# Second mixer of a two-block transformer kernel: an earlier gate chunk, a later second block set, earlier key parts and first scaling, an earlier retention score, later merge transfers

## Chip, cores and metric

The kernel runs on one core of one Trainium2 chip, as a single launch. The metric is the device time of that launch in microseconds (us), the median of three runs. The engines are PE (TensorE, matrix products), DVE (VectorE), ACT (ScalarE), POOL (GpSimd) and SP (SyncE, which here only issues transfers).

## Reference

Two transformer blocks over a sequence of 512 tokens of width 1024, all in fp32. The second block, where the change lies, is a half-weighted SwiGLU, a mixer, a second half-weighted SwiGLU and a norm. Its mixer, cut to what matters:

```python
h = _rmsnorm(x, mix_norm)
(q_a, kc_a, vc_a, ks_a, vs_a, kw_a, vw_a, g_a, q_r, k_r, v_r, g_r, g_merge) = jnp.split(h @ w_in, ...)
nsa_gates = jax.nn.sigmoid(g_a...)
# sparse attention: keys and values of 31 overlapping blocks of 32 tokens, compressed by a small MLP
def compress(tok, w1, w2):
    blk = tok[:, :, cmp_idx] + pos_emb
    return jax.nn.gelu(blk.reshape(...) @ w1) @ w2
kc = _rope(compress(k_cmp, ck_w1, ck_w2), cmp_end); vc = compress(v_cmp, cv_w1, cv_w2)
# scores of q on kc, the key blocks that score best, attention on those and on a window, gated sum
a_out = _nsa(...)
# retention: causal products of q_r and k_r with a decay, times v_r, group norm, times silu(g_r)
r_out = jax.nn.silu(g_r) * _retention(q_r, k_r, v_r, gain)
gate_a, gate_r = jnp.split(jax.nn.sigmoid(g_merge), 2, axis=-1)
x = x + (gate_a * (a_out @ w_branch_nsa) + gate_r * (r_out @ w_branch_ret)) @ w_out
```

## The kernel before

**Products.** Every fp32 product is made of three matmuls on high and low parts (`mm3`, L177 to L179). Activations lie as 8 tiles of 128 x 512 (`xn_hi`, `xn_lo`), and the weights come as a stream of 337 chunks of 512 KB.

**The stream.** SP loads a chunk into one of two buffers `w_raw`; the load of chunk n waits until the low part of chunk n-2 is made. ACT makes the high part (`high_part`, L146, into `w_hi`, a ring of four; it waits for the load and until PE has used chunk n-4). DVE makes the low part (`low_part`, L151, into `w_lo`; it waits for the high part). PE's `ready` waits for the low part. `ahead(part, eng, first, j)` makes the part of chunk first + j + 2. Each engine works through its own list in the order in which the code issues it, so that an instruction that waits holds back all that is behind it on its engine.

**Chunks of the second mixer**, in the order of use: two for the compressed tokens (`b2_cmp`), two for values (`fv`), one for the gates (`fg`), then sixteen called fm+0 to fm+15, two `fk`, and the rest. fm+2c is a chunk of query or key projections (`kq_chunk(c)`, 24 matmuls of 512 columns), fm+2c+1 one of the compressing MLP (8 matmuls of 256 columns on `blk_parts`, L1647 and L1649). `kq_chunk(8)` and `kq_chunk(9)` use the `fk` chunks.

**The start of the mixer.** DVE makes the normed tiles (L224), ACT their high parts (L216), POOL their low parts (L232); this is `scaled_parts`. ACT then copies the compressed tokens across partitions (`ck`, L1553). From `ck` DVE adds the position embedding into `blk`, eight instructions for the keys (`blocks(0)`) and eight for the values (`blocks(1)`), all at L1721. ACT makes the high parts of `blk` (`blocks_high`, L1674), POOL the low parts (L1778). `blk` is cleared on POOL at L1775. The gates are the product with `fg`, a sigmoid on ACT (`gate_fm`, L1681), and a transpose on PE (L1633).

**Rotation.** After `kq_chunk(n)` DVE shuffles and multiplies its bank (L1747, L1749 or L1753, "rotation n" below), and POOL multiplies and adds the sines (L1782, L1787 or L1792). The low parts of the next two chunks stand on DVE ahead of rotation n.

**First scores.** The compressed keys `kc_raw` get high parts on ACT (`high_kc`, L1967) and low parts on POOL (`low_kc`, L2012). PE then makes small scores on them and the first score on the window (L183, L184), runs `kq_chunk(9)`, makes the next score, and transposes the scaled probabilities (L1881). DVE scales those by the gates (`scaled`, L2189 to L2199). `low_q`, `low_k`, `low_v` (L1997, L2005, L2018) are POOL's low parts for queries, keys and values.

**Retention and merge.** In the retention `fill(h, ...)` runs a chunk's matmuls in two parts, and `score(1)` and `values(0)` are products that need parts of the rotated queries and keys (`rk_lo`, POOL L2326). In the merge gates come back from DRAM in four pairs of transfers on POOL's queue (L2633) and `x` in one of 2 MB on ACT's (L2585).

Of the kernel before, what the change touches and what calls it, by code (L numbers as in the profile page):

```python
# [25 lines left out]
S = 512  # L26
# [53 lines left out]
def build_program(nc, stream, xt, cols, tables, rows, decays, pos, w2, out):  # L80
    top = ExitStack()
    with top:
# [125 lines left out]
        def scaled_parts(gain):  # L208
# [4 lines left out]
            def act_part(act):  # L213
                for k in range(KT):
                    act.wait_ge(m["scaled"], b["scaled"] + k + 1)
                    nc.scalar.activation(xn_hi[:, k, :], squares[:, k % 4, :], ACT.Copy).then_inc(m["hi"], 1)  # L216
                    if k == KT // 2:
                        ahead(high_part, act, FIRST["b2_cmp"], 1)

# [1281 lines left out]
        def mixer2(n_mix2, x_done, last_sum, recip_done, opened):  # L1501
# [7 lines left out]
            def tables_in(pool):  # L1509
                pool.wait_ge(*x_done)  # L1510
# [147 lines left out]
            def act_part(act):  # L1658
# [17 lines left out]
                for j in range(2):  # L1676
                    ahead(high_part, act, fv, j)
                ahead(high_part, act, fg, 0)
                blocks_high(0)
                finished(act, fg, 0)  # L1680
                nc.scalar.activation(gate_fm[0:48, :], banks[3][0:48, :], ACT.Sigmoid).then_inc(t["gate"], 1)  # L1681
                for c in range(8):
                    if c == 1:
                        blocks_high(1)
                    ahead(high_part, act, fm, 2 * c)
                    ahead(high_part, act, fm, 2 * c + 1)
# [11 lines left out]
                    if c == 7:  # L1698
                        act.wait_ge(t["kc"], 4)
                        high_kc(0)  # L1700
                        cross_q(act, 0)
# [7 lines left out]
            def dve_part(dve):  # L1709
# [14 lines left out]
                for j in range(2):  # L1724
                    ahead(low_part, dve, fv, j)
                ahead(low_part, dve, fg, 0)
                blocks(0)
                finished(dve, fv, 1)
                for tb in range(TB):
                    nc.vector.tensor_copy(nv[:, tb, :], banks[4 + tb][:, 0:256]).then_inc(t["v"], 1)  # L1730
                blocks(1)
                dve.wait_ge(t["tables"], 128)
                nc.vector.tensor_tensor(fold, ident[:, 0:64], ident[:, 64:P], ALU.add)
                for n in range(10):
# [6 lines left out]
                    for c in ((2 * n, 2 * n + 1) if n < 8 else (n - 8,)):  # L1741
                        ahead(low_part, dve, fm if n < 8 else fk, c)
                    finished(dve, *place_of(n))
# [29 lines left out]
            def pool_part(pool):  # L1773
                pool.wait_ge(*norm_done)
                nc.gpsimd.memset(blk[:], 0.0).then_inc(consts_made, 1)  # L1775
                for kv in range(2):
# [36 lines left out]
        def sparse_attention(start):  # L1813
# [361 lines left out]

            def first_shift(dve):
                compressed_shift(dve, 0)
                biased(dve, 0)

            def dve_part(dve):  # L2180
                dve.wait_ge(t["pad"], 1)
                dve.wait_ge(t["gates"], 1)

                def scaled(U):

                    i, (j, m) = U // 4, units[U % 4]
                    n = slice(4 * (U % 2), 4 * (U % 2) + 4)
# [679 lines left out]
```

## Time and profile before

| what | value |
|---|---|
| median of three runs | 2178.33 us (2175.91 to 2180.74) |
| time of the profiled execution | 2178.4 us |
| its span | 2176.6 us |
| PE busy | 2128.0 us, 98% of the span |
| DVE, ACT, POOL busy | 1188.5, 895.4, 461.5 us |
| second mixer to merge | from about 1120 to 1760 us of the span |

PE is busy for 98% of the span. A stretch is read by asking where PE stands idle, which engine let it go on, what that engine did before, and which clock PE was granted after the idle time. A busy PE at a granted clock of 0.50 does half the work in the same time.

### The profile page before, as it was taken

The page shows a single profiled execution, that of the slowest core. Times are in us where ns is not written, and L with a number is a line of the kernel's source. Part 1 is how long each engine was busy: PE and PEld are TensorE (multiplying, and loading weights), DVE is VectorE, ACT ScalarE, POOL GpSimd, SP SyncE. Part 2 cuts the span into 40 slices and gives each one's busy share as a digit, 9 for nine tenths or more (in the row PEclk, how much of TensorE's full clock was granted, in tenths as well). Part 3 has the DMA queues.
Part 4 walks back from the last instruction along what each step waited for, and adds up shares of the span by engine and source line. Part 5 has one row for each costly group of instructions (what it writes and reads, how often), then busy time and mean ns, then how long its engine had stood idle before and what let it go on. Part 6 is the DMA issues. An engine that isn't in the chain of part 4 may idle for free.

```text
span 2176.6 us, 28422 instructions
## 1 busy us (share of the span) xinstructions
PE 2128.0 (98%) x9960; PEld 1762.4 (81%) x9960; DVE 1188.5 (55%) x1981; ACT 895.4 (41%) x1542; POOL 461.5 (21%) x359
## 2 busy tenths in 40 slices
PE   8999999999999999999998899999999999999997
PEld 6778888888888888888887788888877788888886
DVE  5467774544442264443277678778768335444324
ACT  4355664422221242222133467676655424222212
POOL 2011344211110042310015501111155313111000
PEclk9999999999999999999999999999999999999999
DMA  5212245333333333333324322222264432333331
GB/s 169 78 54 73 83 144 161 91 93 96 96 106 101 92 87 96 96 96 106 97 91 153 108 60 77 83 73 69 92 201 179 147 97 87 97 96 96 108 97 66
DMA packets 66505, 222.91 MB, mean 102 GB/s; under 512 B 7312, under 2 KB 7568, under 8 KB 66032
## 3 DMA queue, kind: packets, MB, share of 16 engines
q1 hardware_dynamic: 51120, 182.08, 27.9%
q10 hardware_dynamic: 11712, 27.27, 3.4%
q0 software_dynamic: 3584, 12.39, 1.7%
q8 instruction: 54, 0.88, 0.2%
q14 instruction: 35, 0.29, 0.0%
HBM read 202.31 MB, written 18.87 MB: 102 GB/s over the span
## 4 chain that ended last, share of the span: by engine, by line
PE 83%; DVE 8%; POOL 3%; ACT 2%; issue 2%; DMA 2%; DVEq 0%; SPq 0%; POOLq 0%; ACTq 0%
PE bank L177 24%; PE bank L178 24%; PE bank L179 24%; PE bank L183 3%; PE bank L184 2%; POOL hid L541 2%; PE bank L1881 2%; DVE gn_r L2480 1%; DMA w_raw<-stream 1%; DVE w_lo L151 1%; DVE xn_lo L456 1%; ACT w_hi L146 1%; PE bank L677 1%; DMA m_more<-spill_g 1%; DVE squares L224 0%
## 5 line engine op out<-in xcount | busy, mean ns | idle before, releaser
L151 DVE TENSOR_TENSOR w_lo<-w_raw,w_hi 128x1024 fp32r<-128x1024 f32 x337 | 463.9, 1380 | 536.3 <-ACT w_hi L146 535.9
L177 PE MATMUL bank<-xn_hi,w_hi 128*128 128x512 f32 x1624 | 648.1, 399 | 7.0 <-DVE w_lo L151 6.8
L179 PE MATMUL bank<-xn_hi,w_lo 128*128 128x512 f32 x1624 | 634.9, 391 | 0.0
L178 PE MATMUL bank<-xn_lo,w_hi 128*128 128x512 f32 x1624 | 634.6, 391 | 0.0
L146 ACT ACTIVATE w_hi<-w_raw 128x1024 fp32r<-128x1024 f32 x337 | 353.2, 1051 | 391.5 <-PE bank L179 236.3
L177 PEld LDWEIGHTS bank<-xn_hi,w_hi 128*128 128x128 f32 x1624 | 307.1, 189 | 71.0 <-DVE w_lo L151 7.7
L179 PEld LDWEIGHTS bank<-xn_hi,w_lo 128*128 128x128 f32 x1624 | 305.9, 188 | 64.9
L178 PEld LDWEIGHTS bank<-xn_lo,w_hi 128*128 128x128 f32 x1624 | 306.7, 189 | 62.6 <-issue 2.6
L177 PE MATMUL bank<-h_hi,w_hi 128*128 (+1 forms) x528 | 205.8, 390 | 0.0
L179 PE MATMUL bank<-h_hi,w_lo 128*128 (+1 forms) x528 | 205.4, 389 | 0.0
L178 PE MATMUL bank<-h_lo,w_hi 128*128 (+1 forms) x528 | 205.4, 389 | 0.0
L547 POOL TENSOR_TENSOR h_lo<-hid,h_hi 128x512 f32 (+1 forms) x66 | 85.6, 1297 | 564.6 <-ACT h_hi L407 564.6
L407 ACT ACTIVATE h_hi<-hid 128x512 f32 (+1 forms) x66 | 41.7, 632 | 290.4 <-DVE hid L477 290.4
L178 PEld LDWEIGHTS bank<-h_lo,w_hi 128*128 128x128 f32 x528 | 99.1, 188 | 20.9 <-issue 0.2
L177 PEld LDWEIGHTS bank<-h_hi,w_hi 128*128 128x128 f32 x528 | 99.1, 188 | 20.7 <-issue 0.2
L179 PEld LDWEIGHTS bank<-h_hi,w_lo 128*128 128x128 f32 x528 | 99.1, 188 | 20.7
L403 ACT ACTIVATE silu<-silu 128x512 f32<-128x512 f32 x66 | 41.6, 631 | 174.5 <-DVE silu L467 174.5
L473 DVE TENSOR_TENSOR hid<-bank,norm_r 128x512 f32<-128x512 f32 x66 | 45.6, 690 | 112.1 <-PE bank L179 112.1
L2066 ACT ACTIVATE npt_hi<-bank 128x512 fp32r<-128x512 f32 (+3 forms) x128 | 48.6, 431 | 70.9 <-PE bank L1881 70.9
L2037 ACT ACTIVATE nprob<-nprob,small 128x128 f32<-128x128 f32 (+3 forms) x128 | 70.8, 555 | 16.9 <-DVE small L2173 16.4
L2205 DVE TENSOR_TENSOR npt_lo<-bank,npt_hi 128x512 fp32r<-128x512 f32 (+3 forms) x128 | 56.7, 484 | 35.2 <-ACT npt_hi L2066 35.2
L467 DVE TENSOR_TENSOR silu<-bank,norm_r 128x512 f32<-128x512 f32 x66 | 45.6, 691 | 45.2 <-PE bank L179 45.1
(414 smaller groups left out, 3120.5 us busy)
## 6 DMA issues: line engine op xcount, KB each, us to landing
w_raw<-stream SPq DMA_DIRECT2D x337, 512.0 KB, 3.7
spill_g<-gate_out ACTq DMA_DIRECT2D x16, 256.0 KB, 2.0
m_more<-spill_g POOLq DMA_DIRECT2D x3, 1024.0 KB, 12.7
x<-xt SPq DMA_DIRECT2D x4, 512.0 KB, 6.5
x<-xt ACTq DMA_DIRECT2D x1, 2048.0 KB, 9.4
spill_x<-x ACTq DMA_DIRECT2D x1, 2048.0 KB, 6.3
spill_ga<-ga_out ACTq DMA_DIRECT2D x8, 256.0 KB, 2.1
spill_rv_hi<-rv_hi_out ACTq DMA_DIRECT2D x8, 256.0 KB, 2.4
```

Source lines behind the costliest of these rows:

```text
L146: nc.scalar.activation(w_hi[:, slot, :], w_raw[:, slot % 2, :], ACT.Copy).then_inc(split_hi, 1)
L151: nc.vector.tensor_tensor(w_lo[:, slot, :], w_raw[:, slot % 2, :], w_hi[:, slot, :], ALU.subtract).then_inc(split_lo, 1)
L177: nc.tensor.matmul(to, a_hi, b_hi, start=start, stop=False, skip_group_check=True)
L178: nc.tensor.matmul(to, a_hi, b_lo, start=False, stop=False, skip_group_check=True)
L179: return nc.tensor.matmul(to, a_lo, b_hi, start=False, stop=stop, skip_group_check=True)
L183: nc.tensor.matmul(to, both, first, start=start, stop=False, skip_group_check=True)
L467: nc.vector.tensor_tensor(silu[:, t, :], banks[bank][:], norm_r[:], ALU.mult).then_inc(s["scaled"], 1)
L473: nc.vector.tensor_tensor(hid[:, t, :], banks[bank][:], norm_r[:], ALU.mult).then_inc(s["scaled"], 1)
L547: nc.gpsimd.tensor_tensor(h_lo[:, bass.ds(i * 2 * S + t * S, S)], hid[:, t, :], h_hi[:, bass.ds(i * 2 * S + t * S, S)], ALU.subtract).then ...
L2037: nc.scalar.activation(at, at, ACT.Exp, bias=neg_top[:, n:n + 1], scale=0.125, accum_out=total[:, n:n + 1]).then_inc(s["exp"], 1)
L2066: nc.scalar.activation(npt_hi[:, KOFF[kb]:KOFF[kb + 1]], banks[4 + kb % 2][:, 0:S - kb * P], ACT.Copy).then_inc(s["hi"], 1)
L2205: nc.vector.tensor_tensor(npt_lo[:, at], banks[4 + kb % 2][:, 0:S - kb * P], npt_hi[:, at], ALU.subtract).then_inc(s["lo"], 1)
```

## The change

- ACT makes the high part of the gate chunk `fg` between the seventh and eighth normed tile, and no longer behind the copies of `ck`. After them come the high part of fm+0, `blocks_high(0)`, the high part of fm+1, and the sigmoid. `blocks_high(1)` moves from behind the high part of fm+3 to behind that of fm+5.
- DVE makes the low part of `fg`, then `blocks(0)`, the low part of fm+0, the copies of the values, the low part of fm+1. `blocks(1)` moves behind rotation 1, ahead of the low part of fm+6.
- POOL clears `blk` ahead of the eight table transfers, which now wait for the last tile of `x` and not the first, and makes the low parts of the values' blocks ahead of rotation 2's sines.
- On ACT `high_kc` moves between the high parts of the two `fk` chunks, from behind both; `low_kc` moves on POOL ahead of `low_v` and one rotation earlier. On DVE the first `scaled` (`first_scaled`, the fourth of `nsa_first`) moves ahead of rotation 9.
- In the retention `score(1)` moves from behind the first chunk's `fill` into its middle.
- In the merge the third and fourth pair of gate transfers are issued by POOL between its sums, and the load of `x` by ACT after the eighth of sixteen steps.

No instruction's size changes. The diff, cut to its core (a function `scaled` that is moved without a change is left out):

```diff
@@ scaled_parts, ACT
                         ahead(high_part, act, FIRST["b2_cmp"], 1)
+                    if k == KT - 2:
+                        ahead(high_part, act, FIRST["b2_v"], 0)
@@ tables_in
-                pool.wait_ge(*x_done)
+                pool.wait_ge(x_done[0], x_done[1] + KT - 1)
+                nc.gpsimd.memset(blk[:], 0.0).then_inc(consts_made, 1)
@@ prepare, ACT
-                for j in range(2):
-                    ahead(high_part, act, fv, j)
+                ahead(high_part, act, fv, 1)
+                blocks_high(0)
                 ahead(high_part, act, fg, 0)
-                blocks_high(0)
...
-                    if c == 1:
+                    if c == 2:
                         blocks_high(1)
                     ahead(high_part, act, fm, 2 * c)
+                    if c == 7:
+                        act.wait_ge(t["kc"], 4)
+                        high_kc(0)
                     ahead(high_part, act, fm, 2 * c + 1)
...
                     if c == 7:
-                        act.wait_ge(t["kc"], 4)
-                        high_kc(0)
                         cross_q(act, 0)
@@ prepare, DVE
-                for j in range(2):
-                    ahead(low_part, dve, fv, j)
-                ahead(low_part, dve, fg, 0)
+                ahead(low_part, dve, fv, 0)
                 blocks(0)
+                ahead(low_part, dve, fv, 1)
                 finished(dve, fv, 1)
...
-                blocks(1)
+                ahead(low_part, dve, fg, 0)
...
+                    if n == 9:
+                        nsa_first[3](dve)
                     finished(dve, *place_of(n))
...
+                    if n == 1:
+                        blocks(1)
@@ prepare, POOL
-                pool.wait_ge(*norm_done)
-                nc.gpsimd.memset(blk[:], 0.0).then_inc(consts_made, 1)
...
+                blocks_low(0)
                 for n in range(10):
+                    if n == 2:
+                        blocks_low(1)
...
                     if n == 6:
+                        low_kc(pool, 0, 4)
+                    if n == 7:
                         finished(pool, fm, 7)
                         low_v(pool, 0)
-                    if n == 7:
-                        low_kc(pool, 0, 4)
@@ sparse_attention
+            def first_scaled(dve):
+                dve.wait_ge(t["gates"], 1)
+                scaled(dve, 0)
...
-                scaled(0)
                 for U in range(UNITS):
@@ retention, PE
                     if h:
                         values(h)
+                    else:
+                        score(pe, 1)
                     fill(h, slot, range(4, KT)).then_inc(used, 1)
                     if h == 0:
-                        score(pe, 1)
@@ merge_two, ACT and POOL
-                act.dma_start(x[:], x_d.rearrange("p (k s) -> p k s", s=S)).then_inc(x_back, 16)
...
+                    if n == KT:
+                        act.dma_start(x[:], x_d.rearrange("p (k s) -> p k s", s=S)).then_inc(x_back, 16)
...
-                for T in (0, 2, 4, 6):
+                for T in (0, 2):
                     second_gates_to(T)
                 for T in range(KT):
+                    if T in (1, 3):
+                        second_gates_to(T + 3)
```

DVE's list at the start of the mixer, before, from the last copies into `ck` on. The three low parts behind them are those of `fg`, fm+0 and fm+1; `nv` is the copy of the values.

```order
L1559 TENSOR_TENSOR ck<-bank,norm_r 128x512 x2
L151 TENSOR_TENSOR w_lo<-w_raw,w_hi 128x1024 x3
L1721 TENSOR_TENSOR blk<-ck,col 64x8x31 x8
L1730 COPY nv<-bank 128x256 x4
L1721 TENSOR_TENSOR blk<-ck,col 64x8x31 x8
L1733 TENSOR_TENSOR small<-ident 128x64
L151 TENSOR_TENSOR w_lo<-w_raw,w_hi 128x1024 x2
L1747 STREAM_SHUFFLE swapped<-bank 128x512
```

The same list of the changed kernel, from the low part of `fg` on; line numbers are shifted by a few.

```order
L151 TENSOR_TENSOR w_lo<-w_raw,w_hi 128x1024
L1724 TENSOR_TENSOR blk<-ck,col 64x8x31 x8
L151 TENSOR_TENSOR w_lo<-w_raw,w_hi 128x1024
L1732 COPY nv<-bank 128x256 x4
L151 TENSOR_TENSOR w_lo<-w_raw,w_hi 128x1024
...
L151 TENSOR_TENSOR w_lo<-w_raw,w_hi 128x1024 x2
L1751 STREAM_SHUFFLE swapped<-bank 128x512
L1757 TENSOR_TENSOR nqk<-bank,nsa_c 64x512 x2
L1724 TENSOR_TENSOR blk<-ck,col 64x8x31 x8
L151 TENSOR_TENSOR w_lo<-w_raw,w_hi 128x1024 x2
```

The second group of eight has moved from ahead of the low parts of fm+2 and fm+3 to ahead of those of fm+6 and fm+7. ACT's list around the gates, before:

```order
L1553 ACTIVATE ck<-ck 64x512 x4
L146 ACTIVATE w_hi<-w_raw 128x1024 x3
L1674 ACTIVATE blk_parts<-blk 128x16x64
L1681 ACT_TABLE_LOAD
L1681 ACTIVATE gate_fm<-bank 48x512
L146 ACTIVATE w_hi<-w_raw 128x1024 x2
L1674 ACTIVATE blk_parts<-blk 128x16x64
```

And of the changed kernel:

```order
L1556 ACTIVATE ck<-ck 64x512 x4
L146 ACTIVATE w_hi<-w_raw 128x1024
L1677 ACTIVATE blk_parts<-blk 128x16x64
L146 ACTIVATE w_hi<-w_raw 128x1024
L1683 ACT_TABLE_LOAD
L1683 ACTIVATE gate_fm<-bank 48x512
L146 ACTIVATE w_hi<-w_raw 128x1024 x4
L1677 ACTIVATE blk_parts<-blk 128x16x64
L146 ACTIVATE w_hi<-w_raw 128x1024 x6
```

The second `blk_parts` now stands behind four high parts (fm+2 to fm+5), and that of fm+6 right behind it. DVE's list at the first scaling, before:

```order
L151 TENSOR_TENSOR w_lo<-w_raw,w_hi 128x1024
L1747 STREAM_SHUFFLE swapped<-bank 128x512
L1749 TENSOR_TENSOR nqk<-bank,nsa_c 128x512
L1770 COPY vc_raw<-bank 128x256
L2189 TENSOR_SCALAR small<-small 128x4
L2191 RECIPROCAL small<-small 128x4
L2193 TENSOR_TENSOR small<-small,gates 128x4
L2199 TENSOR_SCALAR nprob<-nprob,small 128x128
```

And of the changed kernel:

```order
L151 TENSOR_TENSOR w_lo<-w_raw,w_hi 128x1024
L2189 TENSOR_SCALAR small<-small 128x4
L2191 RECIPROCAL small<-small 128x4
L2193 TENSOR_TENSOR small<-small,gates 128x4
L2199 TENSOR_SCALAR nprob<-nprob,small 128x128
L2199 TENSOR_SCALAR nprob<-nprob,small 128x256
L2199 TENSOR_SCALAR nprob<-nprob,small 128x384
L2199 TENSOR_SCALAR nprob<-nprob,small 128x512
L1751 STREAM_SHUFFLE swapped<-bank 128x512
L1753 TENSOR_TENSOR nqk<-bank,nsa_c 128x512
L1776 COPY vc_raw<-bank 128x256
```

The scaling has changed places with rotation 9 and the copy of `vc_raw`.

## Rows read from the trace of the kernel before

**Rows 1.** The page's first part: busy us, share, instructions of each engine.
```profile
PE 2128.0 (98%) x9960; PEld 1762.4 (81%) x9960; DVE 1188.5 (55%) x1981; ACT 895.4 (41%) x1542; POOL 461.5 (21%) x359
```
**Rows 2.** PE's waits, 1140 to 1260: releaser, total us, times, longest us.
```profile
PE bank L177 <- DVE w_lo L151: 6.8, 4, 4.1
PE bank L183 <- POOL kc_a L2012: 4.3, 1, 4.3
PE bank L1633 <- ACT gate_fm L1681: 2.3, 1, 2.3
PE bank L1881 <- DVE nprob L2199: 2.0, 1, 2.0
```
**Rows 3.** PE's timeline: start us, us, engine, line, [idle before].
```profile
1153.41 0.50 PE L177 MATMUL bank<-xn_hi,w_hi 128*128 128x512 f32 x1 [1.44 <-DVE w_lo L151]
...
1172.95 0.80 PE L177 MATMUL bank<-xn_hi,w_hi 128*128 128x512 f32 x1 [4.13 <-DVE w_lo L151]
...
1188.57 0.40 PE L177 MATMUL bank<-xn_hi,w_hi 128*128 128x512 f32 x1
...
1194.99 0.40 PE L177 MATMUL bank<-xn_hi,w_hi 128*128 128x512 f32 x1
...
1233.66 0.36 PE L183 MATMUL bank<-kc_a,nq 128*128 128x32 f32 x1 [4.28 <-POOL kc_a L2012]
...
1251.30 0.78 PE L177 MATMUL bank<-xn_hi,w_hi 128*128 128x512 f32 x1
```
**Rows 4.** Stretches: us, PE, PEld, DVE, ACT, POOL busy, PEclk, DMA, GB/s.
```profile
1172.95:1178.75 5.80, 5.80 (x14) 4.54 (x15) 5.72 (x7) 1.06 (x1) 3.84 (x3) 0.50 0.48 138
1233.66:1240.16 6.50, 6.50 (x26) 6.21 (x27) 2.63 (x10) 0.00 (x0) 2.46 (x2) 0.50 0.00 0
```
**Rows 5.** DVE's timeline at the start of the mixer.
```profile
1158.34 1.23 DVE L151 TENSOR_TENSOR w_lo<-w_raw,w_hi 128x1024 fp32r<-128x1024 f32 x1 [3.85 <-ACT w_hi L146]
1159.48 4.39 DVE L1721 TENSOR_TENSOR blk<-ck,col 64x248 f32<-64x248 f32 x8
...
1165.35 6.15 DVE L1721 TENSOR_TENSOR blk<-ck,col 64x248 f32<-64x248 f32 x8
...
1171.67 4.52 DVE L151 TENSOR_TENSOR w_lo<-w_raw,w_hi 128x1024 fp32r<-128x1024 f32 x2
...
1178.55 2.18 DVE L151 TENSOR_TENSOR w_lo<-w_raw,w_hi 128x1024 fp32r<-128x1024 f32 x1
```
**Rows 6.** ACT's timeline there.
```profile
1148.32 2.60 ACT L1553 ACTIVATE ck<-ck 64x512 f32<-64x512 f32 x4
...
1163.90 1.06 ACT L1674 ACTIVATE blk_parts<-blk 128x1024 fp32r<-128x1024 f32 x1 [5.59 <-DVE blk L1721]
```
**Rows 7.** POOL's timeline there.
```profile
1150.10 1.81 POOL L1775 MEMSET blk<- 128x2048 f32 x1
...
1172.67 2.45 POOL L1778 TENSOR_TENSOR blk_parts<-blk,blk_parts 128x1024 fp32r<-128x1024 f32 x1 [5.28 <-ACT blk_parts L1674]
```
**Rows 8.** POOL's timeline around the compressed keys.
```profile
1226.70 1.30 POOL L1787 TENSOR_TENSOR nqk<-nqk,swapped 128x512 f32<-128x512 f32 x1
...
1233.26 0.25 POOL L2012 TENSOR_TENSOR kc_a<-kc_raw,kc_b 64x32 fp32r<-64x32 f32 x1
```
**Rows 9.** DVE's timeline at the first scaling.
```profile
1247.17 0.58 DVE L2189 TENSOR_SCALAR small<-small 128x4 f32<-128x4 f32 x1
...
1249.19 1.29 DVE L2199 TENSOR_SCALAR nprob<-nprob,small 128x128 f32<-128x128 f32 x4
```
**Rows 10.** PE's waits, 1580 to 1700.
```profile
PE bank L177 <- DVE w_lo L151: 1.6, 1, 1.6
PE bank L177 <- POOL rk_lo L2326: 1.2, 1, 1.2
```
**Rows 11.** Transfers 1670 to 1692: queue, number, KB each, median us to landing.
```profile
w_raw<-stream SPq DMA_DIRECT2D x3, 512.0 KB, 10.6
```
**Rows 12.** The same of the whole span, from the page's last part.
```profile
w_raw<-stream SPq DMA_DIRECT2D x337, 512.0 KB, 3.7
```

More of the change, by code:

```diff
@@ L1773, in pool_part, with blocks_low @@
             def pool_part(pool):
-                pool.wait_ge(*norm_done)
-                nc.gpsimd.memset(blk[:], 0.0).then_inc(consts_made, 1)
-                for kv in range(2):
+                def blocks_low(kv):
                     pool.wait_ge(t["hi"], kv + 1)
@@ L2174, in biased, with scaled @@
                                         ALU.mult).then_inc(s["negated"], 1)
+            def scaled(dve, U):
+                i, (j, m) = U // 4, units[U % 4]
+                n = slice(4 * (U % 2), 4 * (U % 2) + 4)
+                dve.wait_ge(s["exp"], 4 * U + 4 + z["exp"])
+                nc.vector.tensor_scalar(nguard[:, n], total[:, n], 1e-20, None, ALU.max).then_inc(s["guard"], 1)
+                dve.wait_ge(s["guard"], 2 * U + 1)
+                nc.vector.reciprocal(nguard[:, n], nguard[:, n]).then_inc(s["guard"], 1)
+                dve.wait_ge(s["guard"], 2 * U + 2)
+                nc.vector.tensor_tensor(inverse[:, n], nguard[:, n], gates[:, :, i * 6 + 3 * j + 1 + m],
+                                        ALU.mult).then_inc(s["inverse"], 1)
+                dve.wait_ge(s["inverse"], U + 1 + z["inverse"])
+                for qb in range(TB):
+                    at = nprob[:, U % 2, scores_rows(qb)]
+                    n = 4 * (U % 2) + qb
+                    nc.vector.tensor_scalar(at, at, inverse[:, n:n + 1], None, ALU.mult).then_inc(s["scaled"], 1)
             def first_shift(dve):
@@ L2178, in first_shift @@
                 biased(dve, 0)
+            def first_scaled(dve):
+                dve.wait_ge(t["gates"], 1)
+                scaled(dve, 0)
             def dve_part(dve):
                 dve.wait_ge(t["pad"], 1)
[L2182 to L2187, printed above, removed]
-                    dve.wait_ge(s["exp"], 4 * U + 4 + z["exp"])
-                    nc.vector.tensor_scalar(nguard[:, n], total[:, n], 1e-20, None, ALU.max).then_inc(s["guard"], 1)
-                    dve.wait_ge(s["guard"], 2 * U + 1)
-                    nc.vector.reciprocal(nguard[:, n], nguard[:, n]).then_inc(s["guard"], 1)
-                    dve.wait_ge(s["guard"], 2 * U + 2)
-                    nc.vector.tensor_tensor(inverse[:, n], nguard[:, n], gates[:, :, i * 6 + 3 * j + 1 + m],
-                                            ALU.mult).then_inc(s["inverse"], 1)
-                    dve.wait_ge(s["inverse"], U + 1 + z["inverse"])
-                    for qb in range(TB):
-                        at = nprob[:, U % 2, scores_rows(qb)]
-                        n = 4 * (U % 2) + qb
-                        nc.vector.tensor_scalar(at, at, inverse[:, n:n + 1], None, ALU.mult).then_inc(s["scaled"], 1)
                 def lows(U, blocks):
@@ L2269, in dve_part @@
                     if U + 1 < UNITS:
-                        scaled(U + 1)
+                        scaled(dve, U + 1)
                     ahead(low_part, dve, fn, U)
@@ L2297, in sparse_attention @@
             staged = (high_q, high_k, high_kc, high_v, high_vc, low_q, low_k, low_kc, low_v, low_vc, centring, cross_q)
-            return act_part, pe_part, dve_part, pool_part, retain[4], staged, (first_scores, first_exps, first_shift)
+            return act_part, pe_part, dve_part, pool_part, retain[4], staged, (first_scores, first_exps, first_shift, first_scaled)
         def retention(nsa):
```

## Prediction

> **What bounds the kernel now.** First the page: PE is busy 2128.0 of 2176.6 us [rows 1], so a change can only bring what PE stands idle or works at half clock. Next PE's waits in the stretch that the diff touches. From 1140 to 1260 there are four waits for a low part of weights (6.8 us, the longest 4.1), one of 4.3 for the low parts of the compressed keys, one of 2.3 for the gates' sigmoid, one of 2.0 for the scaled probabilities [rows 2]; later 1.2 for `rk_lo` and 1.6 for a low part in the merge [rows 10]. Together 18.2 us. The timeline gives their places: 1.44 ahead of the gate chunk, 4.13 ahead of `kq_chunk(1)`, 4.28 ahead of the small scores [rows 3]. Then the clock: behind the 4.13 PE is busy for 5.80 us at a granted clock of 0.50, behind the 4.28 for 6.50 us [rows 4]. That is the lower of two levels (1.2 for 2.4 GHz), so 2.9 and 3.25 us were lost there. Last, what DVE did ahead of the 4.13: from 1159.48 to 1171.5 it set both halves of `blk` (4.39 and 6.15) with 1.5 of copies between, and only then made the low parts that PE wanted (4.52 for two) [rows 5].
>
> **Part A: gate chunk and second block.** The sum has to follow DVE, in the order of the changed list. The copies of `ck` end at 1150.9 [rows 6]. Low part of `fg`, 1.23 (the undisturbed row): 1152.2. PE's wait of 1.44 there shrinks to about 0.4, since it came free at 1153.41 - 1.44 = 1152.0 [rows 3]. `blocks(0)` 4.39: 1156.6. Low part of fm+0 1.23: 1157.8, ready as PE ends `fg` (below). The copies 1.5: 1159.3. Low part of fm+1, beside POOL's low parts of the first block, 2.2 as in the row of 2.18: 1161.4 [rows 5]. ACT's high part of the first block ends at 1157.7 (1.06) [rows 6], so the sigmoid no longer waits for it and the wait of 2.3 goes. From here the stream sets the pace: the load of fm+3 starts when fm+1's low part is done, lands 3.7 later [rows 12], takes 1.06 on ACT (a pass of the same size as rows 6 show) and 1.23 on DVE: 1167.4. The low part of fm+2 lies ahead of that, near 1164, so the wait of 4.13 before `kq_chunk(1)` goes. Rotation 0 with the gates' copy, 2.36 (from 1176.19, the end of the two low parts, to 1178.55) [rows 5]: 1169.8. Low parts of fm+4 and fm+5, beside POOL's sums, 4.5 as the two before: 1174.3. Rotation 1, 2.0: 1176.3. **Now `blocks(1)` stands in the way**: 6.15 [rows 5], beside POOL's sums of rotation 1, as its row stood beside POOL's subtraction: 1182.4. Its high part on ACT 1.06, then the high part of fm+6 behind it in ACT's list 1.06: 1184.5. Low part of fm+6 beside POOL's subtraction of the second block (2.45) [rows 7], 2.2 to 3.4 (the two of 4.52 less 1.2): 1187.2.
>
> PE meanwhile: `fg`, as long as a `kq_chunk` alone, 1152.3 to 1157.8; a `kq_chunk` with its MLP chunk takes 1194.99 - 1188.57 = 6.4 [rows 3]; the transposes 0.5. So `kq_chunk(1)` starts at 1164.8, `kq_chunk(2)` waits about 0.7 for its low part (1172), and at 1178.4 PE is ready for `kq_chunk(3)`, whose low part comes at 1187.2. A **new wait of 8.8 us** takes the place of 1.44, 2.3 and 4.13. Behind it I put 3.0 lost to the clock, as behind the two long waits of rows 4. `kq_chunk(4)` then starts at 1187.2 + 6.4 + 3.0 = 1196.6 and not at 1194.99: 1.6 late. Two small waits for low parts further on (6.8 - 4.13 - 1.44 = 1.2) go, since PE is no longer ahead of the stream. **A = +0.4 us.** Bounds: `blocks(1)` undisturbed is 4.39, 1.8 sooner; the low part at 2.2 another 1.2 sooner: -2.6. Beside two sums of POOL and not one subtraction, each taking another 1.8 as the row did: +1.8, and a half clock twice as long another 3: together +5, of which I take +3.5 into the range since both would have to come.
>
> For the contention there is a rule. The 6.15 row is 1.8 over the 4.39 one, with one POOL subtraction beside it. The Trainium skill (SBUF — State Buffer, "Who interferes with whom") says that a DVE instruction with two SBUF inputs and a GpSimd instruction that reads SBUF share one port pair, an exclusive lock for a whole instruction. By it POOL's two sums would hold up `blocks(1)` twice, and A would be about +2 in place of +0.4.
>
> The clearing of `blk` (1.81) [rows 7] moves beside DVE's low parts of the compressed branch near 1125, which are on the way to the normed tiles. No row shows a clearing beside such work; the bounds are 0 and its whole 1.81. I take 0: the clearing reads nothing that DVE needs, and the eight table transfers behind it on POOL are wanted only by rotation 0, some 40 us later. The same page and section say that a GpSimd instruction that only writes does not contend with a two-input DVE instruction: 0 by the rule, 1.8 if the lock held for it.
>
> **Part B: key parts and first scaling.** PE is done with `kq_chunk(8)` and the fold at 1233.66 - 4.28 = 1229.4 [rows 3]. In POOL's list `low_kc` now follows the sum that ends at 1228.0; its two instructions of 0.25 end near 1228.6 [rows 8]. That is 0.8 ahead of PE, so the wait of 4.28 goes, and with it the 3.25 at half clock: 7.5 earlier for the first scores and all that follows them. On DVE the first scaling then comes ahead of rotation 9, but PE cannot use that alone: `kq_chunk(9)` ends and the next score is made at about 1240.8, and the turn of the probabilities writes a bank which rotation 9 has to leave. The low part ahead of both moves with the scores, to about 1239.5. The scaling took 3.3 beside POOL (1247.17 to 1250.48, 1.29 of it for the four products) [rows 9]; I take 2.0 now, since POOL gets its share of rotation 9 only behind it. Rotation 9 adds 1.3 (two thirds of rotation 1's 2.0, which has one instruction more): 1242.8. So a wait of 2.0 stays where 1.98 was, for another releaser, and the next chunk starts near 1243.9, one turn later, and not at 1251.30 [rows 3]. **B = -7.4.** Bounds: the remaining wait gone too, -9.4; the scaling at 3.3 and 0.6 more behind it, -5.5.
>
> **Part C: retention score.** A chunk of 24 matmuls takes 5.5 us (24 of the 28 shares of 512 columns in the 6.4 above). `score(1)` in the middle of the first `fill` comes half of that, 2.7 us, sooner, and with it ACT's and POOL's work on the next `rk_lo`; the wait of 1.2 goes [rows 10]. The steps behind it come 1.2 sooner too and may meet their own releasers: I allow 0.9 of it as a bound. **C = -1.1**, bounds -1.2 and -0.3.
>
> **Part D: merge.** A load of weights took 10.6 us to land in the merge's first stretch, with 4 MB of gates and 2 MB of `x` under way, against 3.7 over the span [rows 11, 12]. With half the gates and all of `x` issued later it lands up to 6.9 us sooner, more than the 1.6 that PE waited [rows 10]. The later transfers are due eight and more chunks of 5.5 us after the start, against a landing of about 10, so they hide. SP's queue is not touched; ACT's and POOL's lists each get one issue between steps that PE does not wait for. **D = -1.5**, bounds -1.6 and -0.5.
>
> **Sum.** Against the profiled execution, 2178.4 us (its median is 2178.33, so nothing is corrected): 0.4 - 7.4 - 1.1 - 1.5 = -9.6, **2168.8 us**. By the bounds: A -2.6 to +3.5, the clearing 0 to 1.8, B -9.5 to -5.5, C and D -2.8 to -0.8. All at one end give 2163.5 and 2177.4; all four at once are unlikely, so the forecast's own range is 2164.5 to 2173.5.
>
> **Rivals.**
> (1) *The new wait before `kq_chunk(3)` does not come*, because DVE is done with `blocks(1)` early enough. Then PE starts that chunk at 1178.4, not 1188.57: A = -10.2 - 1.2, and the time is 2178.4 - 11.4 - 10.0 = 2157. Against it: DVE has the same work ahead of fm+6's low part in both orders and stood idle for little (3.85) [rows 5].
> (2) *The change does not do what it says* in B: `low_kc` is late because POOL's sums before it slip by over 0.8 us. Then 4.28 becomes a smaller wait, the clock falls all the same, and B is about -2 in place of -7.4: 2174.2. For it: POOL's list there is one sum of 1.3 behind the other [rows 8], and beside DVE its instructions took longer, 2.45 [rows 7].
> (3) *Slower*: PE is granted 0.50 for long behind a wait twice as long as those of rows 4. Each us at 0.50 loses 0.5; 3.0 are in the sum already. To come out 4.4 us slower than before takes 14 us more lost, that is 28 us more at 0.50, from `kq_chunk(3)` to `kq_chunk(8)`: about 2183. Against it: behind both waits of rows 4 PE worked on without a break and had its clock back after some 6 us.
>
> **How the numbers follow.** A difference under 0.2% (4.4 us) cannot be told from none. Forecast 0.70; rival 1 0.12; rival 2 0.11; rival 3 0.04; the rest 0.03. Faster: the forecast, rival 1 and a third of rival 2, 0.85. Same: 0.10; slower 0.05. The range takes the forecast's bounds, rival 2's time and the upper part of rival 1: 2161.5 to 2174.5.
>
> **What would show it.** In the profile of the changed kernel: one wait of 6 to 10 us for a low part about 36 us after `ck`'s copies, where DVE stands in `blk` and POOL in its sums, with a stretch at 0.50 behind it; no wait for the sigmoid; no wait for `kc_a`; a wait of some 2 us at the first turn whose releaser is rotation 9; no wait for `rk_lo`; a weight load in the merge landing in about 4 us. If the long wait is missing, A was wrong and rival 1 holds; if `kc_a` still ends a wait, B was.

## The result and the profile after

| | before | changed |
|---|---|---|
| median of five runs | 2180.43 us | 2168.29 us |
| lowest and highest | 2175.91, 2182.81 | 2166.97, 2169.62 |
| ratio, 95% interval | | 0.9947 (0.9933 to 0.9962) |
| span of the profiled execution | 2176.6 us | 2166.5 us |

The kernel is 0.53% faster, 11.6 us by the ratio (8.3 to 14.6); the forecast was 2168.8 us. The first part of the page of the changed kernel, beside [rows 1]:

```profile
PE 2125.5 (98%) x9960; PEld 1761.5 (81%) x9960; DVE 1182.4 (55%) x1981; ACT 894.9 (41%) x1542; POOL 462.9 (21%) x359
```

PE's busy time falls by only 2.5 us and the span by 10.1: what went was mostly idle time. PE's waits of the changed kernel, first 1120 to 1265, beside [rows 2]:

```profile
PE bank L177 <- DVE w_lo L151: 8.9, 3, 8.2
PE bank L1889 <- DVE nqk L1753: 2.5, 1, 2.5
PE bank L177 <- POOL xn_lo L234: 1.0, 2, 0.6
```

and 1560 to 1700, beside [rows 10]:

```profile
PE bank L2385 <- ACT gn_sq L2455: 0.7, 2, 0.4
PE bank L177 <- issue: 0.4, 1, 0.4
```

The waits for the sigmoid, `kc_a`, `nprob`, `rk_lo` and in the merge are gone. In their place there is one of 8.2 us for a low part, and at the first turn one of 2.5 whose releaser is rotation 9. The timeline says where (PE, beside [rows 3]):

```profile
1153.52 0.50 PE L177 MATMUL bank<-xn_hi,w_hi 128*128 128x512 f32 x1 [0.25 <-DVE w_lo L151]
...
1173.13 0.50 PE L177 MATMUL bank<-xn_hi,w_hi 128*128 128x512 f32 x1 [0.40 <-DVE w_lo L151]
...
1188.06 0.80 PE L177 MATMUL bank<-xn_hi,w_hi 128*128 128x512 f32 x1 [8.23 <-DVE w_lo L151]
...
1242.20 0.98 PE L1889 MATMUL bank<-ident,nprob 128*128 128x128 f32 x7 [2.48 <-DVE nqk L1753]
```

1188.06 is the first matmul of `kq_chunk(3)`. Ahead of it on DVE, beside [rows 5], and on ACT, beside [rows 6]:

```profile
1153.38 4.36 DVE L1724 TENSOR_TENSOR blk<-ck,col 64x248 f32<-64x248 f32 x8
...
1164.51 1.23 DVE L151 TENSOR_TENSOR w_lo<-w_raw,w_hi 128x1024 fp32r<-128x1024 f32 x1 [1.98 <-ACT w_hi L146]
1167.32 1.23 DVE L151 TENSOR_TENSOR w_lo<-w_raw,w_hi 128x1024 fp32r<-128x1024 f32 x1 [1.57 <-ACT w_hi L146]
...
1177.28 6.11 DVE L1724 TENSOR_TENSOR blk<-ck,col 64x248 f32<-64x248 f32 x8
1185.46 3.68 DVE L151 TENSOR_TENSOR w_lo<-w_raw,w_hi 128x1024 fp32r<-128x1024 f32 x2 [2.07 <-ACT w_hi L146]
```
```profile
1183.42 1.06 ACT L1677 ACTIVATE blk_parts<-blk 128x1024 fp32r<-128x1024 f32 x1 [9.96 <-DVE blk L1724]
1184.38 1.99 ACT L146 ACTIVATE w_hi<-w_raw 128x1024 fp32r<-128x1024 f32 x2
```

This is the chain of the prediction: `blocks(1)` from 1177.28 to 1183.39, its high part, the high part of fm+6, the low part of fm+6. The same trace also shows two places where DVE stood idle, 1.98 and 1.57 us, ahead of the low parts of fm+2 and fm+3.

**Where the time went, stage by stage.** The table takes the same matmul in each trace and gives the time between two of them. "Chunks" runs from the normed tiles (1144.6 in the trace of before) to the fold ahead of the first scores (1228.6), "scores" from there to 1260, "retention" from 1583.8 to 1665.6, "merge" from there to 1701.6.

| us | start | chunks | scores | retention | merge |
|---|---|---|---|---|---|
| before | 1144.61 | 83.98 | 31.29 | 81.82 | 36.04 |
| changed | 1145.90 | 82.27 | 23.77 | 81.47 | 34.23 |
| difference | +1.3 | -1.7 | -7.5 | -0.4 | -1.8 |

The four stages give -11.4. The start is 1.3 us later although of the whole change only the clearing of `blk`, at 1126, lies ahead of it, and that distance is there from 372 us on. The sum is the span's -10.1. In the traces of all kernels here the start lies anywhere from 1144.6 to 1151.6, with the same matmuls ahead of it. So single times of two kernels can't be compared to better than some us, and the experiments below are read by stage.

A stage has a spread too. Six traces have the changed kernel's code in the scores' stage (the changed kernel, e1, e2, e9, e10 and e11) and take 22.30 to 23.83 us there; three have that of before (before, e7, e8) and take 30.97 to 31.45. Part of the spread is the clock: the changed kernel was granted 0.50 for 3.4 us behind the wait at the first turn, and e10, behind a wait of 2.2 there, was not. The first row is of the changed kernel, the second the whole stage of e10 (columns as in [rows 4]):

```profile
1243.10:1246.50 3.40, 3.40 (x10) 2.64 (x10) 2.68 (x10) 2.06 (x7) 1.53 (x2) 0.50 0.02 5
```
```profile
1229.84:1252.14 22.30, 20.04 (x115) 16.91 (x114) 14.68 (x49) 10.17 (x28) 9.76 (x10) 1.00 0.16 48
```

### The profile page after: what moved, and what is told of

Same layout as the page of the kernel before. It is cut to its first block, busy times and chain, and to the rows that moved or that the text cites. A ratio compares the mean times of both kernels' runs of the same rounds, so it can differ in the third digit from the quotient of the medians.

```text
span 2166.5 us, 28422 instructions
## 1 busy us (share of the span) xinstructions
PE 2125.5 (98%) x9960; PEld 1761.5 (81%) x9960; DVE 1182.4 (55%) x1981; ACT 894.9 (41%) x1542; POOL 462.9 (21%) x359
## 4 chain that ended last, share of the span: by engine, by line
PE 86%; DVE 7%; POOL 2%; ACT 2%; issue 2%; DMA 1%; DVEq 0%; SPq 0%; POOLq 0%; ACTq 0%
PE bank L177 25%; PE bank L179 25%; PE bank L178 25%; PE bank L183 3%; PE bank L184 3%; POOL hid L543 2%; PE bank L1889 2%; DVE w_lo L151 1%; DMA w_raw<-stream 1%; DVE gn_r L2491 1%; DVE xn_lo L458 1%; PE bank L679 1%; PE bank L905 1%; POOL hid L1238 1%; DVE squares L226 0%
## 5 line engine op out<-in xcount | busy, mean ns | idle before, releaser
L151 DVE TENSOR_TENSOR w_lo<-w_raw,w_hi 128x1024 fp32r<-128x1024 f32 x337 | 458.6, 1364 | 529.4 <-ACT w_hi L146 527.0
L2045 ACT ACTIVATE nprob<-nprob,small 128x128 f32<-128x128 f32 (+3 forms) x128 | 70.8, 556 | 10.6 <-DVE small L2181 10.1
```

Of the source, the lines that this page charges most:

```text
L151: nc.vector.tensor_tensor(w_lo[:, slot, :], w_raw[:, slot % 2, :], w_hi[:, slot, :], ALU.subtract).then_inc(split_lo, 1)
L2045: nc.scalar.activation(at, at, ACT.Exp, bias=neg_top[:, n:n + 1], scale=0.125, accum_out=total[:, n:n + 1]).then_inc(s["exp"], 1)
```

## Experiments

Seven kernels whose times are not given below ran once: e3 took 2171.65 us, e6 2175.96, e7 2183.46, e8 2176.41, e9 2175.37, e10 2168.69 and e11 2169.54.

**e1: the second block's high part (ACT) and low part (POOL) one step later.**

```diff
-                    if c == 2:
+                    if c == 3:
                         blocks_high(1)
...
-                    if n == 2:
+                    if n == 3:
                         blocks_low(1)
```

> The changed kernel with one step more: the high part of the second block on ACT stands behind the high parts of fm+6 and fm+7 and no longer ahead of them (POOL's low part one rotation later); blocks(1) on DVE stays where it is. Theory (DVE's eight instructions hold back the low part of fm+6, ACT's order adds to it): the low part of fm+6 comes right behind blocks(1), at about 1184.6 in place of 1187, so the wait of 8.2 us before kq_chunk(3) shrinks to 5 to 6 us. Rival a (ACT's order alone makes the wait): it falls under 1 us. Rival b (the load of fm+6 comes late whatever the order): it stays at 8.

PE at `kq_chunk(3)`:

```profile
1187.01 0.80 PE L177 MATMUL bank<-xn_hi,w_hi 128*128 128x512 f32 x1 [4.88 <-DVE w_lo L151]
```

8.23 became 4.88, with 2166.46 us in one run. The 4.9 that stay are DVE's eight instructions and the low part behind them. The other 3.3 came from ACT making the block's high part first and from POOL's subtraction beside the low part; the run moves both and does not part them. Both rivals fall. The chunks' stage gains only 2.4 of the 3.3 (79.91), because `kq_chunk(3)` itself now takes 9.35 us and took 8.30: the shorter wait lost more to the clock.

**e2: the second block in three pieces** (`blocks` takes the numbers of the instructions that it issues).

```diff
-                    if n == 1:
-                        blocks(1)
+                    if n in (1, 2, 3):
+                        blocks(1, {1: (0, 1), 2: (2, 3, 4), 3: (5, 6, 7)}[n])
...
-                    if c == 2:
+                    if c == 4:
                         blocks_high(1)
...
-                    if n == 2:
+                    if n == 4:
                         blocks_low(1)
```

> The changed kernel with blocks(1) split over rotations 1, 2 and 3 (two, three and three instructions), its high part on ACT ahead of fm+8's successor pair (behind the high part of fm+9) and its low part on POOL ahead of rotation 4's sines. Theory (a block of 6 us on DVE is the cause, and DVE has 1 to 2 us to spare in each rotation): the wait of 8.2 us before kq_chunk(3) falls to under 2 us, smaller ones of 0.5 to 2 us come before kq_chunk(4) and kq_chunk(5), and the kernel is 3 to 8 us faster than the changed one (about 2161 to 2165). Rival (DVE has no spare time in these rotations, the work is only moved): waits of together 6 us or more remain and the time stays within 2 us of 2168.

2165.82 us, 0.9932 of before (0.9915 to 0.9948). PE's waits and DVE's pieces:

```profile
PE bank L177 <- DVE w_lo L151: 2.7, 4, 1.3
PE bank L1650 <- POOL blk_parts L1784: 2.3, 1, 2.3
```
```profile
1179.85 2.07 DVE L1726 TENSOR_TENSOR blk<-ck,col 64x248 f32<-64x248 f32 x2
...
1186.66 3.25 DVE L1726 TENSOR_TENSOR blk<-ck,col 64x248 f32<-64x248 f32 x3
...
1193.43 3.23 DVE L1726 TENSOR_TENSOR blk<-ck,col 64x248 f32<-64x248 f32 x3
```

The wait before `kq_chunk(3)` fell to 0.70, but 2.3 came for the block's low part, which now is late for its first use, and 1.3 before `kq_chunk(4)`. With smaller ones, for rotation 9 (0.9), for `pre` (0.5) and for `kc_a` (0.2), PE's waits behind the normed tiles come to 6.6, as the rival had it; but the chunks' stage is 79.38 us, 2.9 under the changed kernel, and the time 2.5 under it. So neither theory nor rival holds in full. An instruction that takes 0.55 alone (4.36 for eight) takes 1.0 to 1.1 in these places, beside POOL's sums.

**e3: the first scaling put back.**

```diff
-                    if n == 9:
-                        nsa_first[3](dve)
...
                 nc.vector.tensor_copy(vc_raw[:], banks[6][:, 192:448].rearrange("p (g d) -> p g d", g=2)
                                       ).then_inc(t["kc"], 1)
+                nsa_first[3](dve)
```

> The changed kernel with the first scaling put back behind rotation 9 and the copy of vc_raw; the key parts stay sooner. Theory (PE needs both the scaling and rotation 9, so their order brings nothing): PE's wait at the first turn of the probabilities is 2 to 3.5 us as now (2.5), with nprob as releaser, and the stage ends within 1 us of the changed kernel. Rival (the earlier scaling is worth the old wait of 2.0): the wait is 4.5 us or more.

```profile
PE bank L1888 <- DVE nprob L2198: 3.3, 1, 3.3
```

The wait is 3.3 in place of 2.5, and the stage of the scores 24.96 in place of 23.77. Both traces have a stretch of 3.4 us at 0.50 behind the turn, so the order of scaling and rotation 9 is worth 1.2 us (1.1 against e11), a little over what the theory allowed. The rival's wait of 4.5 did not come.

**e4: scaling and rotation 9 ahead of the low part before them.**

```diff
-                    for c in ((2 * n, 2 * n + 1) if n < 8 else (n - 8,)):
+                    for c in ((2 * n, 2 * n + 1) if n < 8 else (n - 8,) if n == 8 else ()):
...
+                ahead(low_part, dve, fk, 1)
                 dve.wait_ge(t["kv"], 3)
```

> The changed kernel with the first scaling and rotation 9 ahead of the low part that stands before them on DVE (that of the second chunk behind kq_chunk(9)). Theory (the remaining wait of 2.5 at the turn is DVE's idle time of 3.6 behind ACT plus that low part): scaling and rotation end about 2.4 us sooner, the wait falls under 0.7 us, and the next chunk starts 2 to 4 us sooner (the clock's loss behind the wait may go too). Rival: the low part, now late, makes PE wait behind the first fill as long as it gained.

PE's waits from 1120 to 1265 have no row for `nqk` any more; there is this one instead:

```profile
PE bank L1890 <- DVE npt_lo L2217: 0.9, 1, 0.9
```

The stage of the scores is 21.07, 2.7 under the changed kernel (2165.27 us in one run). The wait at the turn is gone, as the theory had it, and 0.9 came back behind the first fill, as the rival had it in kind. Not all of the 2.7 is the order's: e4 has no stretch at 0.50 in this stage, and against e1 and e10, which have none either (22.55 and 22.30), it gains 1.2 to 1.5. Whether the order also takes that stretch away is not shown.

**e5: the second block in DVE's idle places, with e4.**

```diff
+                        if n == 0:
+                            blocks(1, (2 * c, 2 * c + 1))
                         ahead(low_part, dve, fm if n < 8 else fk, c)
...
-                    if n == 1:
-                        blocks(1)
+                    if n in (1, 2):
+                        blocks(1, (2 * n + 2, 2 * n + 3))
...
-                    if c == 2:
+                    if c == 4:
                         blocks_high(1)
...
-                    if n == 2:
+                    if n == 3:
                         blocks_low(1)
```

> The changed kernel with blocks(1) in pairs of instructions: two ahead of the low part of fm+2 and two ahead of that of fm+3, where DVE stands idle for 2.0 and 1.6 us in the changed kernel's trace, two behind each of rotations 1 and 2; its high part on ACT behind that of fm+9, its low part on POOL ahead of rotation 3's sines; and the first scaling and rotation 9 ahead of the low part before them, as in e4. Theory (DVE's idle time ahead of those low parts is the place for the second block): no wait over 1 us before kq_chunk(3) and later chunks, none at the first turn, and a time 6 to 11 us under the changed kernel (2157 to 2162). Rival (the stretch is bound by DVE's sum of work up to kq_chunk(9), wherever the block stands): waits of together 5 us or more come elsewhere between kq_chunk(1) and the turn, and the time is 2162 to 2166, as the sum of e2 and e4 would give at most.

**2158.67 us** in the median of five runs, 0.9913 of before (0.9900 to 0.9927): 9.6 us under the changed kernel by the medians, 7.4 by the ratios. PE's waits, and the pieces on DVE:

```profile
PE bank L177 <- DVE w_lo L151: 3.1, 6, 0.8
PE bank L177 <- POOL xn_lo L234: 1.0, 2, 0.6
PE bank L1894 <- DVE npt_lo L2221: 0.4, 1, 0.4
PE bank L183 <- POOL kc_a L2025: 0.2, 1, 0.2
```
```profile
1161.13 1.08 DVE L1726 TENSOR_TENSOR blk<-ck,col 64x248 f32<-64x248 f32 x2
1162.47 1.23 DVE L151 TENSOR_TENSOR w_lo<-w_raw,w_hi 128x1024 fp32r<-128x1024 f32 x1 [0.26 <-ACT w_hi L146]
1163.73 1.07 DVE L1726 TENSOR_TENSOR blk<-ck,col 64x248 f32<-64x248 f32 x2
...
1175.90 2.06 DVE L1726 TENSOR_TENSOR blk<-ck,col 64x248 f32<-64x248 f32 x2
...
1182.71 2.65 DVE L1726 TENSOR_TENSOR blk<-ck,col 64x248 f32<-64x248 f32 x2
```

No wait is over 0.8. The idle time of 1.98 ahead of a low part is 0.26 now: four of the eight instructions lie where DVE had nothing to do, and take 1.08 for two; the four beside POOL's sums take 2.06 and 2.65. The chunks' stage is 75.89, 6.4 under the changed kernel, the scores' 22.29, 1.5 under; both have a stretch of 3.4 us at 0.50 in the scores' stage. These 7.9 are the edit's; what the profiled execution gained beyond them lies in stages whose code is the same. The rival falls, with waits of 3.7 and not 5 and a time under 2162: what bound the stretch was where the block stood, not DVE's sum of work.

**e6: the key parts alone, on the kernel before** (`high_kc` and `low_kc` as in the diff, nothing else).

> The kernel before with one part of the change: high_kc between the high parts of the two fk chunks, low_kc one rotation sooner and ahead of low_v. Nothing else. Theory: the wait of 4.28 for kc_a and the stretch at 0.50 behind it go (7 to 7.5 us earlier at the first score), and at the turn PE waits 2 to 4 us; the stage behind the turn is 5.5 to 8 us earlier than before. Rival (the gain of this stage needs the earlier scaling too): the wait at the turn grows by 4 us or more and the stage gains under 4.

```profile
PE bank L1882 <- DVE nprob L2200: 3.3, 1, 3.3
PE bank L183 <- POOL kc_a L2013: 0.2, 1, 0.2
```

The scores' stage is 25.34 against 31.29 before: 5.9 of the 7.5 come from the key parts, on POOL two instructions of 0.25 us that no longer stand behind other work. The theory holds and the rival falls. The rest, 1.6, needs the scaling's new place; e3 gave 1.2 for it.

**e7 and e8: the merge's transfers, one kind at a time, on the kernel before.**

> The kernel before with one part of the change: the third and fourth pair of gate transfers of the merge issued by POOL between its sums; the load of x stays at the start. Theory (all transfers share the engines, so taking 2 of 6 MB away shortens the load of weights only in part): the load lands 2 to 5 us sooner, PE's wait in the merge of 1.55 falls to 0 to 0.5. Rival (the 2 MB of x are what the load waits for): the wait stays over 1.

> The kernel before with one part of the change: the load of x issued by ACT after the eighth step of the merge; all four pairs of gate transfers stay at the start. Theory: the load of weights lands 3 to 6 us sooner and the wait of 1.55 falls to 0 to 0.3, so that x alone would have been enough. Rival (the gates are what it waits for): the wait stays over 1.

The two loads of weights issued while the merge starts, in turn of before, of the changed kernel, of e7 and of e8 (transfers, KB each, median us to landing):

```profile
w_raw<-stream SPq DMA_DIRECT2D x2, 512.0 KB, 11.3
```
```profile
w_raw<-stream SPq DMA_DIRECT2D x2, 512.0 KB, 4.6
```
```profile
w_raw<-stream SPq DMA_DIRECT2D x2, 512.0 KB, 9.3
```
```profile
w_raw<-stream SPq DMA_DIRECT2D x2, 512.0 KB, 5.8
```

Gates later alone: the wait is 0.24 and the stage 34.76. `x` later alone: no wait, 34.23, which is the changed kernel's own time. Both theories hold. `x` later would have been enough, and gates later nearly so; the 2 MB that the load shared its time with most were those of `x`. Moving the gates as well brought 1.2 us of landing that PE does not need. How large the gain is depends on the execution of before: e6, whose merge is the old one, waits 2.5 there, takes 38.65 for the stage, and its two loads land in 12.3:

```profile
w_raw<-stream SPq DMA_DIRECT2D x2, 512.0 KB, 12.3
```

**e9: part A undone in the changed kernel** (orders on ACT, DVE and POOL as before, the clearing of `blk` left in its new place).

> The changed kernel with part A undone: the gate chunk's parts, both halves of the block on ACT, DVE and POOL as in the kernel before; the clearing of blk, the key parts, the first scaling, retention and merge as in the changed kernel. Theory (A alone brings 1.7 us, because the new wait of 8.2 replaces three old ones): PE waits again 1.4, 2.3 and 4.1 us, none of 8.2, and kq_chunk(8) starts 1 to 3 us later against the normed tiles than in the changed kernel; the stage of the first scores keeps its gain of 7 us. Rival (A is a loss, the old order was better): kq_chunk(8) starts at the same distance or sooner.

```profile
PE bank L177 <- DVE w_lo L151: 6.9, 5, 4.2
PE bank L1634 <- ACT gate_fm L1682: 2.2, 1, 2.2
```

The old waits are back and none of 8 is there, as expected, and the scores' stage keeps its gain (23.02). The granted clock was 0.95 from 1182 on, where the other traces have 1.00. That cost little where it can be compared: 130.60 us against 130.12 to 130.19 from 1260 to 1390, and 34.24 against 34.23 in the merge. The chunks' stage is 83.44. The four other traces with the old order have 83.98, 83.90, 83.64 and 83.49 (before, e6, e7, e8), the five with the changed order 82.27, 82.37, 82.37, 82.38 and 83.21 (changed, e3, e4, e11, e10). Part A is worth 0.2 to 1.7, 1.2 between the means. The rival, that A is a loss, falls.

**e10: part C undone in the changed kernel.**

> The changed kernel with part C undone: score(1) of the retention behind the first fill again. Theory (C brings 0.2 to 0.4 us, since two waits of 0.4 each came for the one of 1.2): the wait of 1.2 for rk_lo is back, the waits ahead of values(0) and of the first squares are gone, and PE stands 0.1 to 0.5 us later behind the first squares than in the changed kernel. Rival (C brings the 1.1 that was forecast and something else cost 0.8): PE stands 0.9 us or more later.

```profile
PE bank L177 <- POOL rk_lo L2336: 1.2, 1, 1.2
```

The wait of 1.2 is back, and the first part of the retention (1583.8 to 1598.2) takes 14.39 against 14.25 in the changed kernel's trace. But in seven other traces with part C it takes 13.59 to 13.67. So C is worth 0.8 as a rule, nearer to the rival's 0.9 than to the theory's 0.1 to 0.5, and the changed kernel's own trace is the odd one: it alone has the wait of 0.4 without a named releaser. Both expectations were made on that trace.

**e11: the 2 MB load of the retention later.**

```diff
-                act.dma_start(gr_silu[:], gr_d.rearrange("k p s -> p k s")).then_inc(gr_in, 16)
                 for h in range(HEADS):
...
                     ahead(high_part, act, fgm, h)
+                    if h == 0:
+                        act.dma_start(gr_silu[:], gr_d.rearrange("k p s -> p k s")).then_inc(gr_in, 16)
```

> The changed kernel with the 2 MB load of the gates' activations (gr_silu) of the retention issued behind the first high part of that loop in place of ahead of the second pair of value loads. Theory (the wait of 0.4 ahead of values(0), for which the profile names no releaser, is for the first pair of value loads, whose second half landed 0.1 us ahead of it beside that 2 MB): it lands 1 us or more sooner and the wait goes, 0.3 to 0.5 us. Rival (PE's own issue or another semaphore): the wait stays at 0.4 though the load lands sooner.

The wait of 0.4 is gone, but it is also gone in e1 to e5, which do not have this edit, so the run decides nothing. What the traces show: in the changed kernel's trace the second half of the first value load was issued at 1576.51 and landed at 1584.17, 7.7 later and 0.1 ahead of the matmul that needs it; in e3, e4, e5 and e10 it took 5.5 to 5.9. A load that was slow in one execution is the likely cause, not a shown one.

## Why the prediction was right, and where not

**The sum.** The waits that were to go went, the new one came where it was forecast, and the time fell inside the range. That 2168.29 lies 0.5 us from the forecast 2168.8 is in part luck. The change measured is -11.6 by the ratio, 2.0 more than the forecast -9.6, and the median of before is here 2.0 above the 2178.4 that the forecast set out from. In the profiled pair the stages give -11.4, most of the difference in part A, and the later start of this execution takes 1.3 back.

**Part A**, forecast +0.4, measured -1.7 in the profiled pair. The mechanism came as forecast: the three old waits went, one of 8.23 (8.8) came at the forecast place, `blocks(1)` took 6.11 (6.15), and the low part came for fm+6 behind its high part. Three terms were too dear. The wait is 0.6 shorter. The clock took 1.9 and not 3.0: PE at `kq_chunk(3)` was 0.5 us ahead of before and 1.4 behind it when the chunk was over. This is its stretch (columns as in [rows 4]):

```profile
1187.00:1192.00 5.00, 3.94 (x10) 3.13 (x11) 3.44 (x5) 0.03 (x1) 1.87 (x2) 0.51 0.41 147
1192.00:1229.00 37.00, 37.00 (x190) 31.61 (x189) 28.13 (x36) 19.29 (x27) 25.02 (x19) 1.00 0.50 151
```

PE was busy for 3.94 us at the lower level and then had 1.00, though the wait was twice that of [rows 3]: the loss did not grow with the wait. The clock had come down while PE still stood idle, so that 3 us of the low stretch fell into the wait:

```profile
1180.00:1185.00 5.00, 0.00 (x0) 0.00 (x0) 3.33 (x6) 1.58 (x2) 1.89 (x4) 1.00 0.23 52
1185.10:1188.00 2.90, 0.00 (x0) 0.00 (x0) 2.54 (x2) 1.27 (x2) 1.82 (x1) 0.50 0.00 0
```

In e1, where PE waited 4.88, 6.06 us of work lay at the lower level:

```profile
1187.01:1193.07 6.06, 6.06 (x14) 4.81 (x15) 3.50 (x5) 1.14 (x2) 3.97 (x4) 0.50 0.52 173
```

That is against rival 3, which took a longer half clock for a longer wait. The 1.9 is one execution's: in e3, e4, e11 and e10, behind waits of 8.2 to 8.4, `kq_chunk(3)` took 8.40, 8.41, 8.47 and 9.02 us against 6.42 without one, which is 2.0 to 2.6 lost. And the two small waits of together 1.24 that went gave back 1.8, since the first matmuls behind a wait take longer than those in a row (0.50 us against 0.40 at 1215.86 in the trace of before). 0.6, 1.1 and 0.5 are 2.2; forecast and measurement differ by 2.1.

**Contention.** The Trainium skill (SBUF — State Buffer, "Who interferes with whom") has the two-input instructions of DVE and POOL's reads on one lock. The trace of e5 agrees that they hold each other up: two instructions of `blk` take 1.08 where POOL is idle and 2.06 to 2.65 beside its sums. What I had worked out of it, A at +2, is not what came: over the whole of `blocks(1)` DVE lost 1.75, as [rows 5] had it with a single subtraction.

**The clearing of `blk`**, forecast 0 with a bound of 1.8: it cost nothing. Before, then changed, the low parts beside which it now runs, and the clearing itself:

```profile
1124.98 5.39 DVE L514 SCALAR_TENSOR_TENSOR xg_lo<-x,col,xg_hi 128x512 fp32r<-128x512 f32 x8
```
```profile
1126.28 5.38 DVE L516 SCALAR_TENSOR_TENSOR xg_lo<-x,col,xg_hi 128x512 fp32r<-128x512 f32 x8
```
```profile
1126.42 1.81 POOL L1513 MEMSET blk<- 128x2048 f32 x1 [117.69 <-DVE x L509]
```

The same page and section of the Trainium skill say that an instruction of POOL that only writes does not hold up such a DVE instruction; the trace agrees, 5.38 against 5.39.

**Part B**, forecast -7.4, measured -7.5 in the pair. Over all traces with the two codes it is -7.1 to -9.2, so the mechanism is met and the 0.1 is luck. The wait for `kc_a` went, with `low_kc` done 0.15 us ahead of PE and not 0.8, because the second instruction took 1.12 beside DVE and not 0.25:

```profile
1227.53 1.12 POOL L2020 TENSOR_TENSOR kc_a<-kc_raw,kc_b 64x32 fp32r<-64x32 f32 x1
...
1228.73 1.27 POOL L1790 TENSOR_TENSOR swapped<-swapped,nsa_s 128x512 f32<-128x512 f32 x1
```

So rival 2 was nearer than its 0.11 says; in e5 and e6 the wait for `kc_a` is still there, with 0.2. The wait at the turn stayed, for rotation 9, at 2.48 (2.0). The step on the scaling held: ahead of the rotation it takes 1.9 (2.0), behind it, beside POOL, 3.3 as in [rows 9], and e3 and e6 put 1.2 to 1.6 us on that.

**Part C**, forecast -1.1, measured -0.4 in the pair and -0.8 in the other traces, all of it in the first part of the retention (the part behind it takes 67.20 to 67.40 without C and 67.22 to 67.46 with it). That the steps behind it "may meet their own releasers" stood in the bounds and not in the sum, and it came: 0.4 for the values and 0.4 for the squares in the pair, in the other traces the squares alone, within the bound of 0.9.

**Part D**, forecast -1.5, measured -1.8 in the pair, -4.4 against the old merge in e6's trace. e8 shows that `x` later alone gives the changed kernel's time, and e7 that the gates alone give 1.3 of the 1.8.

**The rivals.** Rival 1 (no new wait, 2157) did not come. e5 comes near its time, 2158.67, with the same instructions in other places, but e4's move is in that too: its chunks' stage is 8.1 under before, where the rival had 11.4. The argument against it, that DVE "stood idle for little (3.85)", is read from the list of before. In the changed list DVE stands idle for 2.0 and 1.6 us more, ahead of the low parts of fm+2 and fm+3. The forecast held all the same, because `blocks(1)` stood behind these places and could not use them.

## What to carry to other kernels

When work is moved down an engine's list, add up that list to the next instruction that the bound engine waits for: the waits that go come back at the new place, here 7.9 us as 8.2, unless the work lands in idle time. Idle places of 1 to 2 us that the trace shows ahead of a stream's instructions can hold a long block if it is cut into pieces, and here they were free of the other engine that slowed it. Two instructions of 0.25 us behind 5 us of unhurried work were worth 6 us of 2180, most of it the wait of 4.28 and the half clock behind it: look first at the shortest work that PE waits for, and at what stands ahead of it.

## What the runs showed of the hardware

The loss behind a wait did not follow its length. At the same granted clock of 0.50 it was 2.9 us behind 4.13 in the kernel before, 1.9 behind 8.23 in the changed one, 2.6 behind 8.38 in e10 and 2.9 behind 4.88 in e1. How much of the low stretch falls into the wait itself differs between executions of the same code.

Executions of the same code differ by up to 7 us ahead of the change (start at 1144.6 to 1151.6). The clock has a part in it: over the first 375 us the kernel before was granted 0.99 and e7, whose start is 7.0 later, 0.97. Stages behind the start repeat better, but not all alike: the stretch from 1260 to 1390 took 130.12 to 130.19 in twelve of the thirteen traces (130.60 at a clock of 0.95), and the one from 1390 to 1583.8 took 193.74 to 193.79 in ten, 192.58 and 192.59 in e5 and e11, whose clock did not fall there, and 195.96 in e9.

One execution (e9) was granted 0.95 over hundreds of us, neither of the two usual levels, and lost under 0.5% by it from 1260 to 1390 and in the merge.
